# A two-layer trunk with a top-2-of-8 expert layer: the large experts' down products go from split fp32r to plain fp32, and scatters and split buffers are rearranged

## The chip, the cores and the metric

The kernel runs on one core of a Trainium2 chip. The metric is the device time of one execution in microseconds; the kernel before took 1336.89 us in the median of three runs (1332.23 to 1337.15). TensorE (PE in the profile) does the matmuls, ScalarE (ACT) and VectorE (DVE) move and change data between PSUM and SBUF, GpSimd (POOL) does little here, and SyncE (SP) issues the DMAs that fetch the weights from HBM.

## The reference, cut to what matters

Two layers over 256 frames of width 1024. The first is a mixer and a dense SwiGLU, the second an attention and a layer of eight experts, of which each frame uses two. Only the expert layer matters here:

```python
def swiglu(x, w1, w3, w2):
    return (jax.nn.silu(x @ w1) * (x @ w3)) @ w2

def moe_swiglu(xn, w_router, w1, w3, w2):
    logits = (xf @ w_router).astype(jnp.float32)
    vals, idx = lax.top_k(logits, TOP_K)                  # TOP_K = 2
    gates = jax.nn.softmax(vals, axis=-1)
    ...
    for e in range(N_EXPERTS):                            # 8; w1, w3: 1024 x 2816, w2: 2816 x 1024
        y = y + combine[:, e:e + 1] * swiglu(xf, w1[e], w3[e], w2[e])
```

Everything is float32. The three matrices of an expert are 34.6 MB, the eight experts 277 MB.

## The kernel before

**Experts, slots and phases.** The kernel orders the experts in a sequence q = 0 to 7. An even q has room for 128 frames ("big", 128 slots), an odd one for 64 ("small"); frames beyond that would be done in a loop at the end. The hidden width of 2816 is done in two halves of 1408. A big expert takes them one after the other, as two phases, a small one together in one, so there are 12 phases n = 0 to 11: q0 in phases 0 and 1, q1 in 2, q2 in 3 and 4, q3 in 5, and so on to q7 in 11. `up n` is the gate and up products of a phase (w1 and w3, 16 steps j), `down n` its down products (w2). TensorE works in the order up 0, up 1, down 0, up 2, down 1, up 3, down 2, up 4, and so on: the down stage of a phase comes after the up stage of the next. One pair of experts, big and small, is six stages: up (raw, small), down (big, second half of the expert before), up (big, first half), down (small), up (big, second half), down (big, first half).

**Two ways to multiply.** A big expert's products are made of three single-pass fp32r matmuls each (`product`, L462 to L464): weights and activations are split into a high part (a copy to fp32r) and the rest. ScalarE writes the high part of a weight piece (`split_step_hi`, L713), VectorE the rest (`split_step_lo`, L1658), into one of three buffers `w_hi`, `w_lo` of 2048 columns. A piece of step v is split behind step v - 3, in both engines' written order. A small expert's products are plain fp32 matmuls on the raw piece in the ring, on half of the array's columns each, two beside each other (L1487, L1511).

**The ring of weights.** Two arenas of SBUF, 10240 and 12288 columns, 11.5 MB together, hold pieces of weights in the order of their use. SyncE issues one DMA a piece (`load_step`, L535) as soon as the space is free: for a piece that was split, when VectorE has split it (`lo_done`); for a raw one, when TensorE has used it (`raw_used`). An up piece is 1408 columns in a big phase (704 KB, 0.721 MB) and 2816 in a small one, a down piece 2048 columns, two blocks of w2 (1.049 MB; the last of a half 1024 columns).

**Around the products.** After an up stage ScalarE makes the silu (`silu_up`, L953) and VectorE multiplies (`gate_up`, L2063); then TensorE turns the 11 blocks of activations (`turn_up`, L1445) and ScalarE and VectorE take them to SBUF. This happens within the down stage that follows; its places ("hooks") stand at every second block. `gather` (L1433) collects the frames of the next expert. `way_back` (L1454) turns the matrix of gates, VectorE copies it (`back_out`, L2081), and `scatter` (L1469) spreads an expert's result over the frames, which VectorE adds to `h` (`add_out`, L2098). Each engine works strictly in its written order, and waits on semaphores.

Of the kernel before, what the change touches and what calls it, by code (L numbers as in the profile page):

```python
# [14 lines left out]
P = 128  # L15
EPS = 1e-6
Step = namedtuple("Step", "kind n q a j hook part size big at ends")
# [4 lines left out]
def trunk(nc, x, e_norm1, e_w_in, e_sgu_ln_g, e_sgu_ln_b, e_sgu_w, e_sgu_b, e_conv_w, e_a_log,  # L22
# [90 lines left out]
    STEPS, n_big, n_raw = [], 0, 0  # L113
    for kind, n in WORK:
        q, a = PHASE[n]
        if kind == "up":
            todo = [Step(kind, n, q, a, j, None, (j // 2, j % 2), HALF if big(q) else FF, big(q), 0, False) for j in range(2 * DC)]
        else:
            todo = []
            for half in ((a,) if big(q) else (0, 1)):  # L120
                for j in range(0, HB, 2):
                    at = len(todo)
                    hook = at if big(q) else at // 2 if at % 2 == 0 else None
                    todo.append(Step(kind, n, q, half, at, hook, (j, min(2, HB - j)), min(2, HB - j) * D, big(q), 0, False))
        todo[-1] = todo[-1]._replace(ends=True)
        for st in todo:
            STEPS.append(st._replace(at=n_big if big(q) else n_raw))
            if big(q):
                n_big += 1
            else:  # L130
                n_raw += 1
# [5 lines left out]

    def place_pieces():

        dense_end = {}  # L140
        for i in range(A_MOE):
            dense_end[slot_of(i)] = i
        taken = [(slot * DC * CW, (slot + 1) * DC * CW, "unit", i) for slot, i in dense_end.items()]
        at = slot_of(A_MOE) * DC * CW
        arena = 0 if at < ARENAS[0][1] else 1
        where = []
        for st in STEPS:
            if at + st.size > ARENAS[arena][1]:
                arena = 1 - arena
                at = ARENAS[arena][0]  # L150
            lo, hi = at, at + st.size
            over = [x for x in taken if x[0] < hi and lo < x[1]]
            taken = [x for x in taken if not (x[0] < hi and lo < x[1])]
            for x in over:
                if x[0] < lo:
                    taken.append((x[0], lo, x[2], x[3]))
                if hi < x[1]:
                    taken.append((hi, x[1], x[2], x[3]))
            units = max([x[3] + 1 for x in over if x[2] == "unit"], default=0)
            raws = max([x[3] + 1 for x in over if x[2] == "raw"], default=0)  # L160
            taken.append((lo, hi, "unit", A_MOE + st.at) if st.big else (lo, hi, "raw", st.at))
            where.append((lo, units, raws))
            at = hi
        return where
# [14 lines left out]
    def arrive_end(k):  # L179
        return arrive_base(k) + 16 * sum(arrive_sem(v) == k for v in range(len(STEPS)))  # L180

    seen_units = seen_raws = 0
    for v, st in enumerate(STEPS):
        seen_units, seen_raws = max(seen_units, WHERE[v][1]), max(seen_raws, WHERE[v][2])
        if v < ARRIVE:
            k = arrive_sem(v)
            assert k >= RING or seen_units > dense_last[k]
        else:
            old = STEPS[v - ARRIVE]
            assert (seen_units > A_MOE + old.at) if old.big else (seen_raws > old.at)  # L190
# [12 lines left out]
    with ExitStack() as ctx:  # L203
# [16 lines left out]
        ident = sb("ident", [P, P])  # L220
        ones = sb("ones", [P, P])
# [3 lines left out]
        blk_ones = sb("blk_ones", [P, P])  # L225
        before = sb("before", [P, P])
# [11 lines left out]
        w_hi = [sb(f"w_hi{i}", [P, PIECE], F32R) for i in range(SPLITS)]  # L238
        w_lo = [sb(f"w_lo{i}", [P, PIECE], F32R) for i in range(SPLITS)]
# [90 lines left out]
        m_hi = [put(f"m_hi{k}", [P, HB, P], F32R) for k in range(2)]  # L330
        m_lo = [put(f"m_lo{k}", [P, HB, P], F32R) for k in range(2)]
        assert end[0] <= nc.sbuf_usable_end
        m_raw = [over(odd_at + 4 * HALF * k)[0](f"m_raw{k}", [P, HB, P]) for k in range(2)]
# [3 lines left out]
        r2 = put("r2", [P, 8, TILES, NE])  # L337
        nat = put("nat", [P, 8, NE])
# [4 lines left out]
        assert end[0] <= masks_at + 3 * 4 * P  # L343
# [97 lines left out]
        MOE_SCAT = (5, 0, 1, 2)  # L441
# [26 lines left out]
        def _(sp):  # L468
# [47 lines left out]
            def load_step(v, st, e):  # L516
# [8 lines left out]
                if st.kind == "up":  # L525
                    c, w = st.part
                    cols = slice(st.a * HALF, (st.a + 1) * HALF) if st.big else slice(0, FF)
                    src = (o_moe_w1, o_moe_w3)[w][0][bass.ds(e, 1), c * P:(c + 1) * P, cols].rearrange("e p n -> p (e n)")
                    dst = in_ring(lo, st.size)
                else:  # L530
                    j, nb = st.part
                    rows = slice(st.a * HALF, (st.a + 1) * HALF)
                    src = o_moe_w2[0][bass.ds(e, 1), rows, :].rearrange("e (j p) d -> p (e j) d", p=P)[:, j:j + nb, :]
                    dst = in_ring(lo, st.size).rearrange("p (j d) -> p j d", j=nb)
# [3 lines left out]
            for v, st in enumerate(STEPS):  # L538
                if st.q not in expert_of:
                    if len(expert_of) == 1:  # L540
                        sp.wait_ge(order_ready, 1)
                    expert_of[st.q] = sp.value_load(order_i[0:1, st.q:st.q + 1], min_val=0, max_val=NE - 1)
                load_step(v, st, expert_of[st.q])
# [125 lines left out]
        def _(act):  # L669
# [38 lines left out]
            def split_step_hi(v):  # L708

                st, i = STEPS[v], A_MOE + STEPS[v].at  # L710
                act.wait_ge(ring_in[arrive_sem(v)], arrive_count(v))
                used(act, i - SPLITS)
                act.activation(w_hi[i % SPLITS][:, 0:st.size], in_ring(WHERE[v][0], st.size), ACT.Copy).then_inc(hi_done, 1)  # L713
# [213 lines left out]
            split_step_hi(0)  # L927
            split_step_hi(1)
            norm(3)
            split_step_hi(2)  # L930
# [4 lines left out]
            def gathered(q):  # L935

                for b in range(2):
                    act.wait_ge(gather_done, 2 * q + b + 1)
                    src = ps[:, gather_bank(q, b), :]
                    if big(q):  # L940
                        act.activation(xg_hi[:, 4 * b:4 * b + 4, :], src.rearrange("p (c n) -> p c n", c=4), ACT.Copy)\
                            .then_inc(xgh_ready, 1)
                    else:
                        act.activation(xg_raw[:, 4 * b:4 * b + 2, :], src[:, 0:2 * SMALL].rearrange("p (c n) -> p c n", c=2),
                                       ACT.Copy).then_inc(xgh_ready, 1)
# [9 lines left out]
            def turned_hi(n, parts=range(PARTS)):  # L955

                for b in parts:
# [3 lines left out]
                    if big(PHASE[n][0]):  # L961
                        dst = m_hi[n % 2][:, blocks[0]:blocks[-1] + 1, :]
                    else:
                        src, dst = src[:, 0:2, :], m_raw[n % 2][:, blocks[0]:blocks[0] + 2, :]
                    act.activation(dst, src, ACT.Copy).then_inc(hTh_ready, 1)

            def finished(q):
# [4 lines left out]
                else:  # L972
                    ins = act.activation(y_exp[SMALL:P, 0:512], ps[SMALL:P, 6, :], ACT.Copy)
# [3 lines left out]
            for v, st in enumerate(STEPS):  # L977
                if finished_before(st) is not None:
                    finished(finished_before(st))
                if st.kind == "up" and st.n == 1 and st.j == 0:  # L980
                    silu_up(0)
                    turned_hi(0, (0, 1))
                if st.kind == "up" and st.n == 1 and st.j == 4:
                    turned_hi(0, (2,))
                if st.kind == "down" and st.n + 1 < PHASES:
                    q = PHASE[st.n + 1][0]
                    if st.hook == 0:
                        silu_up(st.n + 1)
                    if st.hook == 1:
                        turned_hi(st.n + 1)  # L990
                    if st.hook == 2 and LAST[q] == st.n + 1 and q + 1 < NE:
# [18 lines left out]
            with act.If(n_more > 0):  # L1010
                with act.Fori(0, n_more) as it:
# [9 lines left out]
        def _(pe):  # L1021
# [426 lines left out]
            def way_back(q):  # L1448

                pe.wait_ge(gated_done, TILES * (q + 1))  # L1450
                if q:
                    pe.wait_ge(scat_added, 4 * (q - 1) + 1)
                for t in range(TILES):
                    last = pe.transpose(ps[0:SLOTS, 5, t * P:(t + 1) * P], sel_w[:, t, :], ident[:, :])  # L1454
                last.then_inc(back_done, 1)

            def scatter(q, parts=range(4)):
                pe.wait_ge(hTl_ready, TURN0 + PARTS * min(LAST[q] + 3, PHASES))
                pe.wait_ge(back_ready, q + 1)
                pe.wait_ge(y_act, q + 1)  # L1460
                pe.wait_ge(y_vec, q + 1)
                for m in parts:
                    t, hf = m // 2, m % 2
                    if big(q):
                        a, y = back[:, t, :], y_exp[:, hf * 512:(hf + 1) * 512]
                    else:
                        rows = slice(hf * SMALL, (hf + 1) * SMALL)
                        a, y = back[rows, t, :], y_exp[rows, 0:512]
                    mm(ps[:, MOE_SCAT[m], :], a, y, start=True, stop=True).then_inc(scat_done, 1)  # L1469

            def up_step(v, st):

                (c, w), o = st.part, 3 * st.part[1]
                if st.big:
                    i = A_MOE + st.at
                    pe.wait_ge(lo_done, i + 1)
                    hi, lo = w_hi[i % SPLITS], w_lo[i % SPLITS]
# [743 lines left out]
```

## Time and profile before

| | |
|---|---|
| median of three runs | 1336.89 us |
| profiled execution, its own time | 1333.27 us |
| its span on the core | 1331.4 us |
| granted TensorE clock, mean | 0.964 |
| TensorE busy | 1216.3 us (91%) |
| VectorE, ScalarE busy | 691.6, 558.0 us |
| from HBM | 349.93 MB, 264 GB/s over the span |
| expert layer, from its first gather to its last product | 558.7 to 1319.2 us |

The expert layer takes 57% of the span. Its DMAs run at 420 to 430 GB/s where they are not held up. Busy shares are averages over stages with different limits, so the stages are read one by one.

### The profile page before, as it was taken

How to read it: one execution, taken by the hardware profiler on the slowest of the kernel's cores; microseconds unless marked ns; L12 is line 12 of the kernel's file. 1: busy time of each engine (PE TensorE's matmuls, PEld its weight loads, DVE VectorE, ACT ScalarE, POOL GpSimd, SP SyncE). 2: the span in 40 equal slices, each digit the busy share in tenths (PEclk: the TensorE clock that was granted, in tenths of full speed). 3: DMA queues.
4: the chain of work that ended last, by engine and by line, in shares of the span. 5: the costliest groups of instructions: out<-in, count | busy, mean ns of one | idle time of the engine just before them, and what ended most of it. 6: DMA issues, size and time to landing. Idle time of an engine off the chain costs nothing.

```text
span 1331.4 us, 15638 instructions
## 1 busy us (share of the span) xinstructions
PE 1216.3 (91%) x6391; PEld 906.7 (68%) x6391; DVE 691.6 (52%) x738; ACT 558.0 (42%) x597; POOL 52.6 (4%) x89
## 2 busy tenths in 40 slices
PE   6999899999999999788897998988998979999976
PEld 5899777888879987677735747537667457486352
DVE  4875545444454454587605848226567046484052
ACT  4661235433444565366404637125455035372041
POOL 7000000000000023000000000000000000000000
PEclk9999789999998999898998999999999989999989
DMA  9521219755553430186699999699997899995992
GB/s 309 175 92 47 96 32 371 235 174 185 190 182 125 153 131 19 63 280 241 239 404 420 363 395 417 266 424 392 354 419 316 343 420 371 368 404 197 426 419 120
DMA packets 107708, 352.05 MB, mean 264 GB/s; under 512 B 7072, under 2 KB 54192, under 8 KB 99440
## 3 DMA queue, kind: packets, MB, share of 16 engines
q1 hardware_dynamic: 106336, 347.11, 68.8%
q0 software_dynamic: 1296, 3.90, 1.0%
q8 instruction: 52, 0.85, 0.3%
q14 instruction: 24, 0.20, 0.0%
HBM read 349.93 MB, written 1.05 MB: 264 GB/s over the span
## 4 chain that ended last, share of the span: by engine, by line
PE 79%; DVE 8%; DMA 7%; ACT 3%; POOL 2%; issue 1%; POOLq 0%; DVEq 0%; ACTq 0%; SPq 0%
PE ps L462 17%; PE ps L463 17%; PE ps L464 17%; PE ps L1487 7%; PE ps L1511 6%; DMA arena_c<-in_o_moe_w_dram 5%; DVE w_lo L1658 4%; PE ps L1433 2%; ACT w_hi L713 2%; PE ps L1469 2%; PE ps L1445 2%; DMA arena_a<-in_o_moe_w_dram 1%; DVE u_act L2063 1%; PE ps L1360 1%; PE ps L1206 1%
## 5 line engine op out<-in xcount | busy, mean ns | idle before, releaser
L1658 DVE TENSOR_TENSOR w_lo<-arena_c,w_hi 128x1408 fp32r<-128x1408 f32 (+2 forms) x96 | 170.0, 1778 | 199.4 <-ACT w_hi L713 199.3
L713 ACT ACTIVATE w_hi<-arena_c 128x1408 fp32r<-128x1408 f32 (+2 forms) x96 | 144.8, 1509 | 228.9 <-DMA arena_c<-in_o_moe_w_dram 154.7
L1658 DVE TENSOR_TENSOR w_lo<-arena_a,w_hi 128x1408 fp32r<-128x1408 f32 (+2 forms) x80 | 138.1, 1732 | 93.1 <-ACT w_hi L713 93.1
L713 ACT ACTIVATE w_hi<-arena_a 128x1408 fp32r<-128x1408 f32 (+2 forms) x80 | 117.5, 1469 | 130.9 <-PE ps L464 67.3
L462 PE MATMUL ps<-w_hi,xg_hi 128*128 128x512 f32 (+1 forms) x384 | 147.2, 383 | 10.3 <-DVE back L2081 6.4
L463 PE MATMUL ps<-w_lo,xg_hi 128*128 128x512 f32 (+1 forms) x384 | 145.7, 379 | 0.0
L464 PE MATMUL ps<-w_hi,xg_lo 128*128 128x512 f32 (+1 forms) x384 | 144.9, 377 | 0.0
L462 PE MATMUL ps<-w_hi,x_hi 128*128 128x512 f32 (+1 forms) x336 | 125.7, 374 | 1.9 <-ACT xn L800 1.7
L464 PE MATMUL ps<-w_hi,x_lo 128*128 128x512 f32 (+1 forms) x336 | 122.9, 366 | 0.0
L463 PE MATMUL ps<-w_lo,x_hi 128*128 128x512 f32 (+1 forms) x336 | 122.8, 366 | 0.0
L1651 DVE TENSOR_TENSOR w_lo<-arena_a,w_hi 128x2048 fp32r<-128x2048 f32 x40 | 91.5, 2290 | 46.9 <-ACT w_hi L706 46.9
L462 PE MATMUL ps<-w_hi,m_hi 128*128 128x512 f32 x176 | 77.6, 441 | 19.6 <-DVE w_lo L1658 19.6
L462 PEld LDWEIGHTS ps<-w_hi,xg_hi 128*128 128x128 f32 x384 | 73.0, 190 | 26.5 <-issue 10.1
L1487 PE MATMUL ps<-arena_c,xg_raw 128*64 128x512 f32 (+1 forms) x432 | 87.5, 558 | 2.8 <-DMA arena_c<-in_o_moe_w_dram 2.8
L706 ACT ACTIVATE w_hi<-arena_a 128x2048 fp32r<-128x2048 f32 x40 | 76.5, 1912 | 27.6 <-PE ps L464 23.9
L462 PE MATMUL ps<-x_hi,w_hi 128*128 128x256 f32 x288 | 83.7, 291 | 3.7 <-DVE x_lo L1644 3.7
L1651 DVE TENSOR_TENSOR w_lo<-arena_c,w_hi 128x2048 fp32r<-128x2048 f32 x25 | 57.3, 2293 | 52.3 <-ACT w_hi L706 52.3
L464 PE MATMUL ps<-x_hi,w_lo 128*128 128x256 f32 x288 | 82.7, 287 | 0.0
L463 PE MATMUL ps<-x_lo,w_hi 128*128 128x256 f32 x288 | 82.7, 287 | 0.0
L464 PEld LDWEIGHTS ps<-w_hi,xg_lo 128*128 128x128 f32 x384 | 73.1, 190 | 11.7
L463 PEld LDWEIGHTS ps<-w_lo,xg_hi 128*128 128x128 f32 x384 | 73.1, 190 | 11.6
L1487 PE MATMUL ps<-arena_a,xg_raw 128*64 128x512 f32 x336 | 69.4, 560 | 6.1 <-DMA arena_a<-in_o_moe_w_dram 6.1
(349 smaller groups left out, 1904.6 us busy)
## 6 DMA issues: line engine op xcount, KB each, us to landing
arena_c<-in_o_moe_w_dram SPq DMA_DIRECT2D x36, 1408.0 KB, 9.9
arena_c<-in_o_moe_w_dram SPq DMA_DIRECT2D x69, 704.0 KB, 9.4
arena_c<-in_o_moe_w_dram SPq DMA_DIRECT2D x46, 1024.0 KB, 9.6
arena_a<-in_o_moe_w_dram SPq DMA_DIRECT2D x59, 704.0 KB, 8.8
arena_a<-in_o_moe_w_dram SPq DMA_DIRECT2D x28, 1408.0 KB, 8.9
arena_a<-in_o_moe_w_dram SPq DMA_DIRECT2D x34, 1024.0 KB, 9.2
arena_c<-in_e_ffn_w_dram SPq DMA_DIRECT2D x36, 512.0 KB, 4.8
arena_a<-in_e_ffn_w_dram SPq DMA_DIRECT2D x30, 512.0 KB, 4.8
```

The source lines that it names most:

```text
L462: pe.matmul(o, a_hi, b_hi, start=first, stop=False)
L463: pe.matmul(o, a_hi, b_lo, start=False, stop=False)
L464: return pe.matmul(o, a_lo, b_hi, start=False, stop=last)
L706: act.activation(w_hi[i % SPLITS][:, :], ring[slot][:, :], ACT.Copy).then_inc(hi_done, 1)
L713: act.activation(w_hi[i % SPLITS][:, 0:st.size], in_ring(WHERE[v][0], st.size), ACT.Copy).then_inc(hi_done, 1)
L1433: last = mm(ps[:, gather_bank(q, c // 4), at:at + n], xn[:, t, c * P:(c + 1) * P], sel_p[:, t, 0:n], start=(t == 0), stop=(t == TILES - 1))
L1445: last = pe.transpose(ps[:, turn_bank(n, b), i * P:(i + 1) * P], u_act[:, j * P:(j + 1) * P], ident[:, :])
L1469: mm(ps[:, MOE_SCAT[m], :], a, y, start=True, stop=True).then_inc(scat_done, 1)
L1487: last = mm(ps[a * SMALL:(a + 1) * SMALL, o + b, 0:n], xg_raw[:, c, :], raw[:, a * HALF + c0:a * HALF + c0 + n], start=(c == 0), stop=(c = ...
L1511: last = mm(ps[hf * SMALL:(hf + 1) * SMALL, 6, :], m_raw[st.n % 2][:, j, st.a * SMALL:(st.a + 1) * SMALL], raw[:, k * D + hf * 512:k * D + ...
L1651: tt(w_lo[i % SPLITS][:, :], ring[slot][:, :], w_hi[i % SPLITS][:, :].bitcast(F32), ALU.subtract).then_inc(lo_done, 1)
L1658: tt(w_lo[i % SPLITS][:, 0:st.size], in_ring(WHERE[v][0], st.size), w_hi[i % SPLITS][:, 0:st.size].bitcast(F32), ALU.subtract).then_inc(lo ...
```

## The change

In words:

- The down products of big experts are one plain fp32 matmul on the raw piece, full width, in place of three on split parts. `m_hi`, `m_lo` go; the turned activations are copied once, by ScalarE, to `m_raw`. VectorE only passes the semaphore on.
- A down step is one block of w2 (j = 0 to 10 in a half), no longer two; a fetched down piece is still two. A small up piece is fetched as two DMAs of 704 KB, no longer one of 1408 KB.
- `w_hi` and `w_lo` are one area of 6144 columns each, which holds four pieces of 1408. Only up pieces of big experts are split. A table `BEHIND` says behind which step a split is issued: behind the step that used the piece whose buffer it takes, or, if that is later, behind the step that frees the ring space its own fetch needs.
- The turn stands at block 3 of a big down stage and block 5 of a small one, the gather at block 5.
- Scatters and ways back stand only in small down stages: for the big expert before, way back at block 7, scatters at 10 and 12; for the small expert before that, at 14, 17 and 19. Their PSUM banks change.
- The routing operations on VectorE in up 0 are spread over steps 2, 5, 8, 11, and part of them goes to up 2. The first turn stands at steps 3 and 7 of up 1, no longer at 0 and 4.

```diff
+            for half in (a,) if big(q) else (0, 1):
+                for j in range(HB):
+                    if j % 2 == 0:
+                        v = new_piece(kind, q, half, (j, min(2, HB - j)), min(2, HB - j) * D, False)
+                    todo.append(Step(kind, n, q, half, len(todo), j, D, False, 0, False, [(v, (j % 2) * D)]))
...
+        for s, st in enumerate(STEPS):
+            if not st.big:
+                continue
+            if at + st.size > SPLIT_ROOM:
+                at = 0
+            last = max(claim(taken, at, at + st.size, A_MOE + st.at))
+            spot[st.at] = (at, last)
+            raws = max(raws_needed[:st.pieces[0][0] + 1])
+            free = step_of.get(last, last - A_MOE)
+            if raws:
+                free = max(free, raw_step[raws - 1])
+            behind.setdefault(free, []).append(s)
+            at += st.size
...
-        MOE_SCAT = (5, 0, 1, 2)
+        SCAT = {q: (5, 4, 0, 1) if big(q) else (2, 5, 4, 0) for q in range(NE - 1)}
+        TURN_AT, GATHER_AT = {True: 3, False: 5}, 5
+        SCAT_AT = {0: ((10, (0, 1)), (12, (2, 3))), 1: ((17, (0, 1)), (19, (2, 3)))}
+        BACK_AT, LAST_BACK_AT = (7, 14), 20
...
-                            last = product(pe, ps[:, 6 + hf, :], m_hi[st.n % 2][:, j, :], m_lo[st.n % 2][:, j, :],
-                                           w_hi[i % SPLITS][:, cs], w_lo[i % SPLITS][:, cs],
-                                           st.a == 0 and j == 0, st.a == 1 and j == HB - 1)
+                (v, off), = st.pieces
+                pe.wait_ge(ring_in[arrive_sem(v)], arrive_count(v))
+                raw = in_ring(WHERE[v][0] + off, D)
+                for hf in range(2):
+                    if big(st.q):
+                        last = mm(ps[:, 6 + hf, :], m_raw[st.n % 2][:, j, :], raw[:, hf * 512:(hf + 1) * 512], start=first, stop=end)
+                        continue
...
                 if st.kind == "down" and st.n + 1 < PHASES:
-                    if st.hook == 0:
+                    if st.j == 0:
                         silu_up(st.n + 1)
...
-                if v + SPLITS < len(STEPS) and STEPS[v + SPLITS].big:
-                    split_step_hi(v + SPLITS)
+                for k in BEHIND.get(s, ()):
+                    split_step_hi(STEPS[k])
```

**Where instructions move.** First ScalarE, at the end of the raw up stage `up 5` (expert 3) and in the big down stage `down 4` behind it. `u_act` is the silu, `m_raw` the turned activations, `ring_in` the semaphore of a piece's arrival. Before:

```order
L713 ACTIVATE w_hi<-arena_a 128x2048 [waits piece_used,ring_in11]
L713 ACTIVATE w_hi<-arena_a 128x2048 [waits piece_used,ring_in12]
L713 ACTIVATE w_hi<-arena_c 128x2048 [waits piece_used,ring_in13]
L953 ACTIVATE u_act<-ps 128x512 [waits hT_done,raw_used]
L953 ACTIVATE u_act<-ps 128x512
L953 ACTIVATE u_act<-ps 128x384
```

Now:

```order
L773 ACTIVATE all_hi<-arena_c 128x1408 [waits piece_used,ring_in13]
L773 ACTIVATE all_hi<-arena_c 128x1408 [waits piece_used,ring_in14]
L773 ACTIVATE all_hi<-arena_c 128x1408 [waits piece_used,ring_in15]
L773 ACTIVATE all_hi<-arena_c 128x1408 [waits piece_used,ring_in16]
L1015 ACTIVATE u_act<-ps 128x512 [waits hT_done,raw_used]
L1015 ACTIVATE u_act<-ps 128x512
```

Three splits of pieces of `down 4` stood ahead of the silu; now four splits of pieces of `up 6` do. VectorE's order there is the same with its own halves of the splits and the gating. The six pieces of `down 4` are fetched ahead of those four.

Second VectorE, in the small down stage `down 5`. `back` is the turned matrix of gates, `h` the additions behind a scatter. Before:

```order
L2063 TENSOR_TENSOR u_act<-u_act,ps 128x384 [waits silu_done]
L2073 TENSOR_TENSOR m_lo_59<-ps,m_hi_57 128x512 [waits hTh_ready] x2
L2073 TENSOR_TENSOR m_lo_59<-ps,m_hi_57 128x384 [waits hTh_ready]
L2098 TENSOR_TENSOR h<-h,ps 128x512 [waits scat_done] x4
L1658 TENSOR_TENSOR w_lo<-arena_a,w_hi 128x1408 [waits hi_done]
L2081 COPY back<-ps 128x256 [waits back_done]
```

Now:

```order
L2125 TENSOR_TENSOR u_act<-u_act,ps 128x384 [waits silu_done]
L2040 TENSOR_SCALAR sel_w<-iota,tab 128x128 x2
L1714 TENSOR_TENSOR all_lo<-arena_c,all_hi 128x1408 [waits hi_done]
L1714 TENSOR_TENSOR all_lo<-arena_c,all_hi 128x1408 [waits hTh_ready,hi_done]
L1714 TENSOR_TENSOR all_lo<-arena_c,all_hi 128x1408 [waits hi_done]
L2137 COPY back<-ps 128x256 [waits back_done]
L1714 TENSOR_TENSOR all_lo<-arena_c,all_hi 128x1408 [waits hi_done]
L2154 TENSOR_TENSOR h<-h,ps 128x512 [waits scat_done] x4
```

The three splits ahead of `back` are of pieces whose ring space is freed by blocks 3, 5 and 5 of this same stage; before, the scatter of the big expert came ahead of any split, with a `back` made in the stage before.

## Rows read from the trace of the kernel before

**Rows 1.** The page's busy times: us, share of the span, instructions.
```profile
PE 1216.3 (91%) x6391; PEld 906.7 (68%) x6391; DVE 691.6 (52%) x738; ACT 558.0 (42%) x597; POOL 52.6 (4%) x89
```
**Rows 2.** Windows: length, busy PE, PEld, DVE, ACT, POOL, clock, DMA share, GB/s; by pair.
```profile
662.65:850.42 187.77, 173.05 (x820) 110.95 (x818) 96.86 (x86) 76.27 (x68) 0.00 (x0) 0.98 0.93 377
850.42:1037.34 186.92, 173.78 (x820) 113.18 (x821) 96.91 (x86) 76.77 (x68) 0.00 (x0) 0.97 0.92 371
1037.34:1225.42 188.08, 175.38 (x819) 114.53 (x821) 96.32 (x84) 76.79 (x68) 0.00 (x0) 0.96 0.91 361
1225.42:1319.20 93.78, 82.98 (x369) 37.51 (x369) 19.93 (x22) 13.74 (x14) 0.00 (x0) 0.96 0.82 339
```
**Rows 3.** The third pair's windows: up 8 (raw), down 7, up 9, down 8 (small), up 10, down 9.
```profile
1037.34:1080.35 43.01, 38.16 (x192) 13.57 (x193) 2.29 (x1) 3.73 (x2) 0.00 (x0) 1.00 0.93 384
1080.35:1108.52 28.17, 23.93 (x111) 19.55 (x112) 18.37 (x20) 15.11 (x17) 0.00 (x0) 0.88 1.02 421
1108.52:1140.93 32.41, 32.41 (x144) 27.52 (x144) 23.52 (x17) 18.02 (x13) 0.00 (x0) 0.95 0.95 350
1140.93:1166.13 25.20, 25.20 (x111) 8.62 (x110) 10.42 (x16) 7.07 (x9) 0.00 (x0) 1.00 0.94 374
1166.13:1197.75 31.62, 30.97 (x146) 26.37 (x145) 25.53 (x17) 23.02 (x17) 0.00 (x0) 1.00 1.01 410
1197.75:1225.42 27.67, 24.72 (x119) 18.90 (x121) 16.18 (x17) 9.85 (x12) 0.00 (x0) 0.94 0.57 211
```
**Rows 4.** PE's waits from 556 us on (total, times, longest); timeline rows with idle time.
```profile
PE ps L1445 <- DVE u_act L2063: 23.9, 9, 4.9
PE ps L462 <- DVE w_lo L1658: 23.5, 10, 4.3
PE ps L462 <- DVE back L2081: 6.4, 3, 2.2
...
573.82 0.50 PE L462 MATMUL ps<-w_hi,xg_hi 128*128 128x512 f32 x1 [1.91 <-DVE w_lo L1658]
...
604.20 1.97 PE L1445 MATMUL ps<-ident,u_act 128*128 128x128 f32 x8 [4.85 <-DVE u_act L2063]
```
**Rows 5.** The chain that ended last, third pair: start, us, what.
```profile
1037.34 28.52 PE ps L1487 x144
...
1066.00 15.06 DMA arena_a<-in_o_moe_w_dram
...
1085.32 1.67 DVE u_act L2063 x3
...
1091.67 0.23 PE ps L463
...
1092.83 3.57 PE ps L1433 x32
```
**Rows 6.** fp32 matmuls: L1271's row (starts of first and last), and chain rows.
```profile
L1271 PE MATMUL ps<-rn,ones x4: 593/593/593, 177.2 to 178.5; 128*128 128x512 f32 x4
...
1031.89 1.06 PE ps L1469 x4
...
1152.10 1.91 PE ps L1469 x4
1154.01 3.58 PE ps L1511 x16
```
**Rows 7.** ScalarE's timeline at the third down piece; DMA of the window 1092 to 1108.
```profile
1081.09 1.91 ACT L713 ACTIVATE w_hi<-arena_a 128x2048 fp32r<-128x2048 f32 x1 [0.65 <-DMA arena_a<-in_o_moe_w_dram]
...
DMA packets 1359, 6.79 MB, mean 425 GB/s; under 512 B 153, under 2 KB 153, under 8 KB 1359
```
**Rows 8.** In down 8: landing of pieces into arena_c; a split on ACT and DVE.
```profile
DMA to landing us min/median/max: 5.1/6.5/8.2
...
1155.00 1.38 ACT L713 ACTIVATE w_hi<-arena_c 128x1408 fp32r<-128x1408 f32 x1 [0.38 <-DMA arena_c<-in_o_moe_w_dram]
...
1160.15 1.62 DVE L1658 TENSOR_TENSOR w_lo<-arena_c,w_hi 128x1408 fp32r<-128x1408 f32 x1
```

More of the change, by code:

```diff
@@ L16 @@
 EPS = 1e-6
-Step = namedtuple("Step", "kind n q a j hook part size big at ends")
+Step = namedtuple("Step", "kind n q a j part size big at ends pieces")
+Piece = namedtuple("Piece", "kind q a part size big last")
 EXP_LN = "natural_log_exp_and_others"
@@ L136, in trunk, with claim @@
     ARRIVE = 18
+    def claim(taken, lo, hi, mark):
+        over = [x for x in taken if x[0] < hi and lo < x[1]]
+        left = [x for x in taken if not (x[0] < hi and lo < x[1])]
+        for x in over:
+            if x[0] < lo:
+                left.append((x[0], lo, x[2]))
+            if hi < x[1]:
+                left.append((hi, x[1], x[2]))
+        taken[:] = left + [(lo, hi, mark)]
+        return [x[2] for x in over]
     def place_pieces():
@@ L146, in place_pieces @@
         where = []
-        for st in STEPS:
-            if at + st.size > ARENAS[arena][1]:
+        for pc in PIECES:
+            if at + pc.size > ARENAS[arena][1]:
                 arena = 1 - arena
                 at = ARENAS[arena][0]
[L151 to L163, printed above, removed]
+            old = claim(taken, at, at + pc.size, (pc.big, (A_MOE if pc.big else 0) + pc.last))
+            units = max([i + 1 for unit, i in old if unit], default=0)
+            raws = max([i + 1 for unit, i in old if not unit], default=0)
+            where.append((at, units, raws))
+            at += pc.size
         return where
@@ L179, in arrive_end @@
     def arrive_end(k):
-        return arrive_base(k) + 16 * sum(arrive_sem(v) == k for v in range(len(STEPS)))
+        return arrive_base(k) + 16 * sum(arrive_sem(v) == k for v in range(len(PIECES)))
     seen_units = seen_raws = 0
-    for v, st in enumerate(STEPS):
+    for v, pc in enumerate(PIECES):
         seen_units, seen_raws = max(seen_units, WHERE[v][1]), max(seen_raws, WHERE[v][2])
@@ L329, in trunk @@
         put, end = over(odd_at)
-        m_hi = [put(f"m_hi{k}", [P, HB, P], F32R) for k in range(2)]
-        m_lo = [put(f"m_lo{k}", [P, HB, P], F32R) for k in range(2)]
+        m_raw = [put(f"m_raw{k}", [P, HB, P]) for k in range(2)]
         assert end[0] <= nc.sbuf_usable_end
-        m_raw = [over(odd_at + 4 * HALF * k)[0](f"m_raw{k}", [P, HB, P]) for k in range(2)]
         put, end = over(masks_at)
@@ L337, in trunk @@
         r2 = put("r2", [P, 8, TILES, NE])
+        assert end[0] <= before_at
+        put, end = over(before_at)
         nat = put("nat", [P, 8, NE])
@@ L342, in trunk @@
         order_i = put("order_i", [1, 8], I32)
-        assert end[0] <= masks_at + 3 * 4 * P
+        assert end[0] <= level_at
+        y_small = over(ones_at)[0]("y_small", [P, 512])
+        back_last = over(level_at)[0]("back_last", [SLOTS, TILES, P])
         table = tab[:, 0:6, :].rearrange("p (k t) n -> p k t n", t=TILES)
@@ new lines, in down_step @@
+            def down_step(st):
+                j = st.part
+                first, end = st.a == 0 and j == 0, st.a == 1 and j == HB - 1
+                (v, off), = st.pieces
+                pe.wait_ge(ring_in[arrive_sem(v)], arrive_count(v))
+                raw = in_ring(WHERE[v][0] + off, D)
[3 more added lines that the diff above has]
+                        continue
+                    last = mm(ps[hf * SMALL:(hf + 1) * SMALL, 6, :], m_raw[st.n % 2][:, j, st.a * SMALL:(st.a + 1) * SMALL],
+                              raw[:, hf * 512:(hf + 1) * 512], start=first, stop=end)
```

345 lines of the change are left out of this document (181 added, 164 removed).

## Prediction

> **What bounds the kernel now.** I read four views. First the page's busy times: TensorE is busy for 91% of the span [rows 1], so whatever leaves it idle or gives it more to do is the time. Then the windows of the expert part, cut where TensorE starts the gate and up products of a 64-slot expert: three stretches of 187.8, 186.9 and 188.1 us, each one pair of experts, and a last one of 93.8 us [rows 2]. Then one such pair by stage [rows 3]. The reader is to see two things there. TensorE idles in four of the six stages (43.01 - 38.16, 28.17 - 23.93, 31.62 - 30.97, 27.67 - 24.72: 12.7 us in all), and its granted clock is below 1 in three: 12% of 28.2, 5% of 32.4 and 6% of 27.7 us are 6.7 us. The DMA share is 0.93 to 1.02 in the first two stages and 0.57 in the last, so the transfers limit only around the 64-slot expert. Last the waits: for the gated activation 23.9 us, for VectorE's half of a split 23.5, for the copy `back` 6.4 [rows 4]. The chain shows where the longest of these come from: a piece issued at 1066.00 lands 15 us later, is split by ScalarE and VectorE, and only then are the activations gated and turned [rows 5].
>
> A pair needs 69.2 MB of weights. At the 425 GB/s of a saturated stretch [rows 7] that is 163 us, so memory alone doesn't bound a pair, before or after.
>
> **TensorE's work.** The down products of the four 128-slot experts are 4 x 22 blocks x 2 column halves = 176 products. Before, each is three single-pass matmuls of 0.233 us (the 0.23 of [rows 5]; its neighbours show 0.23 and 0.24), 0.70 us. Now each is one fp32 matmul, which the trace counts as two instructions. Full-width fp32 rows: four instructions of L1271 start within 1.3 us, 0.433 us apart; in L1469, between matmuls on 64 columns, four take 1.91 us, 0.478 each [rows 6]. I take 0.44, near the pure stream: 0.88 a product, 1.76 us a block, 19.4 us for a half where it was 15.4. That is 352 x 0.44 - 528 x 0.233 = +31.9 us; the two ends are 352 x 0.433 (+29.4) and 352 x 0.478 (+45.2). Gain or nothing is excluded, since both ends lie above 0.70.
>
> The Trainium skill (FP8 and Floating Point Precision, "TensorE Precision Notes") says that true FP32 takes four passes through the array. With a pass at the measured 0.233 us that would be 0.93 a product, +41 us in the sum, between my value and the upper end; the row of L1271, at 0.87, lies under it.
>
> **What goes with the splits.** After the up products of a 128-slot expert, ScalarE and VectorE no longer have three 2048-column pieces to split ahead of gating. The waits there (0.65 for the split, 2.9 for gating, in the stages at 1166 and 1197: [rows 3]) lose their cause; gating takes 1.7 us [rows 5], the silu before it about as long, and TensorE has three blocks, 5.3 us, before it turns. So -3.6 us a pair. The wait for `back` at the start of an up stage, 6.4 / 3 = 2.1 us [rows 4], goes with the way back that moved: -2.1. ScalarE and VectorE are under no load in a down stage now; that by itself is worth nothing.
>
> **The first new wait: gating behind four splits.** Up splits now run four pieces ahead and are issued behind the step that frees their ring space. For the 128-slot expert that follows a 64-slot one these are steps 12 to 14 of the raw up stage. In both engines' order four splits therefore stand ahead of the silu and the gating of the 64-slot expert, and each waits for its piece to land. These pieces are fetched after all six of the down stage in between, though TensorE needs them later. Queued behind them: silu, gating, the turn at block 3 of the down stage, and all of TensorE.
> A ledger from TensorE's start of the raw up stage (t = 0, 1037.34 in the trace): before, the third down piece is split from 1081.09 on [rows 7], t = 43.7. By then 16 x 1.442 + 3 x 1.049 = 26.2 MB must have arrived, of which 7 pieces (10.1 MB) fit in the ring at t = 0; 16.1 MB in 43 us against 384 GB/s x 43 = 16.5 in the stage [rows 3]. So the ledger holds. Now the fourth up piece is what counts: 23.07 + 5.77 (six down pieces) + 4 x 0.721 = 31.7 MB, of which the finer pieces let 15 x 0.721 = 10.8 MB in at t = 0. The rest flows from the first freed step (2.4 us): 2.4 + 20.9 / 0.425 = 51.6, landed at 52.1. ScalarE's split 1.4, VectorE's 1.6 [rows 8], gating 1.7: the turn can start at 56.9. TensorE gets there at 16 x 2.377 (28.52 us for 144 instructions, 12 a step, [rows 5]) + 5.3 = 43.3. It waits 13.6 us, where it now loses about 7 (0.62, 4.24 and 2.13, the 0.62 and 4.24 as 43.01 - 38.16 in [rows 3]). The clock falls in it as now: 3.4 us (12% of 28.17). Bounds: nothing, if pieces were there; 20 us, if the ring is not full at t = 0.
>
> **The second new wait: `back` behind two splits.** In the 64-slot down stage the way back of the 128-slot expert stands at block 7, the first scatter at block 10. VectorE's copy `back` stands behind the splits of pieces whose space is freed by blocks 3 and 5 of this very stage. With the turn (1.4 us), block 5 ends 0.895 x 6 + 1.4 = 6.8 us in (16 instructions of a block's kind in 3.58 us are four blocks: [rows 6]). Two pieces then are issued; the first lands 6.5 us later [rows 8], the second 1.7 after it (0.721 MB at 425 GB/s): 15.0. Split 1.4 and 1.6, copy 0.4: 18.4. TensorE reaches block 10 at 0.895 x 10 + 1.4 + 0.4 = 10.7: 7.7 us of waiting, and 1.7 for the clock (as 6% of 27.67, [rows 3]). Bounds: 4.6 with the shortest landing of [rows 8], 5.1 us, and no second piece behind it; nothing, if the splits found their pieces; above, 9.
>
> **The sum.** One pair from t = 0: raw up 38.0; down 5.3 + 13.6 + turn 1.4 + eight blocks 14.1 + gather 3.5 [rows 5] + clock 3.4, to 79.3; up 30.9; 64-slot down 19.7 + 1.4 + ways back 0.8 + scatters 3.8 and 2.1 (two each of 1.91 and 1.06, [rows 6]) + 7.7 + 1.7, to 147.4; up 30.9; down 19.4 + 1.4 + 3.5: 202.6 us against 187.6. Three pairs: +45.0. The first has one scatter and way back fewer: -2.5. The last stretch has no split to wait for and the DMA has the ring full: 38.0 + 20.8 + 26.8 + 0.4 = 86.0 against 93.8: -7.8. Start of the expert part: the first turn waits 4.85 us now and moves three steps later (-3, with its clock); two waits of 1.9 for splits [rows 4], with the routing operations spread, -2; the first down stage +4.0 - 3.6: together -4.6. The 64 more DMAs of 704 KB cost nothing: such pieces already move at 425 GB/s [rows 7], and SyncE issues them inside its waits; bounds 0 to 2 us. Sum +30.1, from 1333.3 to 1363.4. The median of the runs shown is 3.6 above that execution; I add a part of that and say 1364.
>
> The skill's page DMA: Bandwidth & Descriptors ("Rules for kernel authors") asks for at least 1 MiB in a DMA. By it the halved pieces would be slower. The trace's 704 KB pieces at 425 GB/s do not bear it out, so it gets no chance of its own.
>
> **Rivals.**
> - *Dear fp32 matmuls.* 0.478 us an instruction as between the tiled ones: +13, 1376. For it: the only fp32 rows with changing weights in this part; against it: half of each row's surroundings are another tiling.
> - *Only the first wait.* If the copy `back` is in time (the two pieces land early or the scatter finds VectorE free), 3 x 9.4 us less: 1336, no change. For it: landing is measured on other traffic; against it: the order of VectorE.
> - *Neither wait, the faster side.* If at t = 0 the DMA is some 3.7 MB further on, so that the fourth up piece has landed at 43 and not at 52, gating is in time as well: another 3 x 17.0 less, 1285. It decides from where the four pieces land before TensorE has done three blocks. Against it: the ring's 11.5 MB are full already in my ledger.
>
> **How the numbers follow.** This kernel's measurement can tell 0.5% from no change, 6.7 us. Forecast with both waits 0.60; dear matmuls on top 0.14; only the first wait 0.14 (a third each slower, same, faster, as its sizes scatter); neither 0.12. Slower 0.60 + 0.14 + 0.04 = 0.78, same 0.06, faster 0.16. The range leaves out the 1285 case and the top of the dear one: 1318 to 1388. The likeliest case by itself: 1350 to 1378.
>
> **What would show it.** After a raw up stage: four splits on ScalarE, then silu; a TensorE wait for gating of 12 to 15 us, three times, and none after 128-slot up stages. In the 64-slot down stage: a TensorE wait of 5 to 9 us at the first scatter, for `back`. fp32 down instructions 0.43 to 0.48 us apart. Last stretch 86 us. Wrong would be: the ledger, if the pieces land before 50; the price, if a half takes over 21 us; or a saving I don't see, if TensorE's sum of idle time falls.

## The result and the profile after

| | before | after |
|---|---|---|
| median | 1337.02 us (4 runs) | 1374.37 us (4 runs, 1373.72 to 1375.95) |
| profiled execution, its span | 1331.4 us | 1372.6 us |
| granted TensorE clock, mean | 0.964 | 0.951 |

The ratio is 1.0306, with a 95% interval of 1.0282 to 1.033: the change makes the kernel 3.1% slower. The forecast was 1364 us, with a range of 1318 to 1388. The line numbers below are those of the changed kernel: `product` is L523 to L525, the raw up products L1549, the down products of a 128-slot expert L1562 and of a 64-slot one L1564, the turn L1506, the gather L1494, the scatter L1531; the splits are L773 (ScalarE) and L1714 (VectorE), silu L1015, gating L2125, the copy `back` L2137, SyncE's DMAs L595. In the experiments the same lines stand a few numbers further on (the turn is L1509 in e2, L1512 in e3).

The page's busy row of after, answering to [rows 1] (us, share of the span, instructions):

```profile
PE 1237.1 (90%) x6215; PEld 868.4 (63%) x6215; DVE 574.1 (42%) x646; ACT 475.2 (35%) x549; POOL 52.6 (4%) x89
```

VectorE and ScalarE lost 117 and 83 us of work, and nothing came of it: neither sets the time by its busy share. TensorE got 21 us more, and the span 41. The other half must be idle time.

Windows of after, cut where TensorE starts a 64-slot expert's up products, answering to [rows 2] (length; busy PE, PEld, DVE, ACT, POOL; clock, DMA share, GB/s):

```profile
654.44:860.81 206.37, 178.76 (x765) 103.72 (x767) 63.85 (x54) 55.94 (x56) 0.00 (x0) 0.93 0.86 337
860.81:1066.25 205.44, 180.00 (x775) 103.83 (x777) 67.87 (x63) 56.11 (x56) 0.00 (x0) 0.93 0.84 337
1066.25:1271.50 205.25, 179.32 (x776) 103.72 (x776) 67.34 (x61) 56.12 (x56) 0.00 (x0) 0.94 0.87 339
1271.50:1360.30 88.80, 85.96 (x358) 31.73 (x357) 10.56 (x21) 3.53 (x7) 0.00 (x0) 1.00 0.87 357
```

The three pairs take 617.1 us where they took 562.8 (+54.3). The expert part's first pair starts 8.2 us earlier (654.44 for 662.65), and the last stretch is 5.0 shorter. Less was moved per us (337 to 339 GB/s for 361 to 377): memory waited too.

The second pair by stage, in the order of [rows 3] (up raw, down, up, down small, up, down; the rows of before are its third pair, which is as long as its second within 1.2 us):

```profile
860.81:899.90 39.09, 38.29 (x193) 13.82 (x193) 0.00 (x0) 0.00 (x0) 0.00 (x0) 1.00 1.01 412
899.90:944.20 44.30, 26.40 (x88) 14.79 (x89) 9.98 (x11) 9.74 (x12) 0.00 (x0) 0.77 0.73 286
944.20:975.20 31.00, 31.00 (x146) 26.28 (x147) 20.19 (x13) 17.47 (x14) 0.00 (x0) 1.00 1.02 409
975.20:1010.20 35.00, 28.25 (x113) 9.16 (x111) 15.11 (x21) 7.98 (x10) 0.00 (x0) 0.90 0.67 261
1010.20:1041.00 30.80, 30.80 (x146) 25.57 (x143) 20.23 (x14) 17.22 (x13) 0.00 (x0) 1.00 1.02 420
1041.00:1066.25 25.25, 25.25 (x97) 14.21 (x97) 2.35 (x5) 3.70 (x8) 0.00 (x0) 1.00 0.60 224
```

Four stages have length equal to busy time, or nearly. All of the loss stands in two: the down stage behind the raw up stage (44.3 us for the 28.2 of [rows 3]) and the small down stage (35.0 for 25.2).

TensorE's waits from 556 us on, answering to [rows 4] (engine, line waited for: total, times, longest):

```profile
PE ps L1506 <- DVE u_act L2125: 52.2, 3, 17.9
PE ps L1531 <- DVE back L2137: 21.9, 3, 8.2
PE ps L1549 <- DMA arena_a<-in_o_moe_w_dram: 4.0, 5, 0.9
PE ps L523 <- ACT u_act L1015: 2.9, 1, 2.9
```

Twenty-two short and middling waits (23.9 + 23.5 + 6.4 us) have gone, but for one of 2.9 us, and six long ones have come: three of about 17.4 us for the gating, three of about 7.3 for `back`. The chain of the second pair shows the first (start, us, what):

```profile
900.95 17.42 DMA arena_c<-in_o_moe_w_dram
...
918.39 1.39 ACT all_hi L773
...
919.80 1.62 DVE all_lo L1714
921.43 1.67 DVE u_act L2125 x3
...
923.14 2.61 PE ps L1506 x11
```

ScalarE's timeline there shows who stands in front of whom (in brackets the idle time before, and what ended it; two of the four splits are left out):

```profile
913.38 1.38 ACT L773 ACTIVATE all_hi<-arena_c 128x1408 fp32r<-128x1408 f32 x1 [62.51 <-DMA arena_c<-in_o_moe_w_dram]
...
918.39 1.38 ACT L773 ACTIVATE all_hi<-arena_c 128x1408 fp32r<-128x1408 f32 x1 [0.31 <-DMA arena_c<-in_o_moe_w_dram]
919.68 1.44 ACT L1015 ACTIVATE u_act<-ps 128x512 f32<-128x512 f32 x3
```

ScalarE has been idle for 62.5 us, 13.5 of them after the up stage ended at 899.90 and the silu's input was complete. The silu isn't late because ScalarE is busy, but because four splits stand ahead of it in the written order, each waiting for a piece that TensorE needs only a stage later. In the small down stage VectorE's timeline shows the same with `back`:

```profile
986.26 1.62 DVE L1714 TENSOR_TENSOR all_lo<-arena_c,all_hi 128x1408 fp32r<-128x1408 f32 x1 [8.41 <-ACT all_hi L773]
988.88 3.16 DVE L1714 TENSOR_TENSOR all_lo<-arena_c,all_hi 128x1408 fp32r<-128x1408 f32 x2 [0.99 <-ACT all_hi L773]
991.96 0.42 DVE L2137 COPY back<-ps 128x256 f32<-128x256 f32 x1
```

Three splits stand ahead of `back`, as the order listing has it. The chain to it, in the same stage, which TensorE starts at 974.86:

```profile
978.68 6.15 DMA arena_c<-in_o_moe_w_dram
...
986.14 1.03 ACT m_raw L1023 x2
...
987.46 1.40 ACT all_hi L773
...
988.88 3.16 DVE all_lo L1714 x2
992.04 0.34 DVE back L2137
```

### The profile page after: what moved, and what is told of

The parts are those of the page before. It is cut to its first block, busy times and chain, and to the rows that moved or that the text cites. A ratio compares the mean times of both kernels' runs of the same rounds, so it can differ in the third digit from the quotient of the medians.

```text
span 1372.6 us, 15350 instructions
## 1 busy us (share of the span) xinstructions
PE 1237.1 (90%) x6215; PEld 868.4 (63%) x6215; DVE 574.1 (42%) x646; ACT 475.2 (35%) x549; POOL 52.6 (4%) x89
## 4 chain that ended last, share of the span: by engine, by line
PE 80%; DMA 9%; DVE 4%; ACT 2%; POOL 2%; SPq 1%; issue 1%; POOLq 0%; DVEq 0%; ACTq 0%
PE ps L523 15%; PE ps L525 15%; PE ps L524 15%; PE ps L1562 10%; PE ps L1549 7%; PE ps L1564 5%; DMA arena_a<-in_o_moe_w_dram 5%; DMA arena_c<-in_o_moe_w_dram 4%; PE ps L1494 2%; PE ps L1531 2%; SPq L595 1%; PE ps L1506 1%; DVE all_lo L1714 1%; PE ps L1421 1%; PE ps L1267 1%
## 5 line engine op out<-in xcount | busy, mean ns | idle before, releaser
L1714 DVE TENSOR_TENSOR all_lo<-arena_a,all_hi 128x1408 fp32r<-128x1408 f32 x60 | 97.0, 1623 | 168.9 <-ACT all_hi L773 168.0
L1714 DVE TENSOR_TENSOR all_lo<-arena_c,all_hi 128x1408 fp32r<-128x1408 f32 x68 | 110.0, 1623 | 100.9 <-ACT all_hi L773 100.7
L523 PE MATMUL ps<-all_hi,xg_hi 128*128 128x512 f32 (+1 forms) x384 | 146.4, 381 | 2.9 <-ACT u_act L1015 2.9
L524 PE MATMUL ps<-all_lo,xg_hi 128*128 128x512 f32 (+1 forms) x384 | 144.4, 376 | 0.0
L525 PE MATMUL ps<-all_hi,xg_lo 128*128 128x512 f32 (+1 forms) x384 | 143.8, 374 | 0.0
L773 ACT ACTIVATE all_hi<-arena_a 128x1408 fp32r<-128x1408 f32 x60 | 82.8, 1383 | 174.7 <-DMA arena_a<-in_o_moe_w_dram 147.4
L773 ACT ACTIVATE all_hi<-arena_c 128x1408 fp32r<-128x1408 f32 x68 | 94.0, 1386 | 113.4 <-DMA arena_c<-in_o_moe_w_dram 72.2
L523 PE MATMUL ps<-all_hi,x_hi 128*128 128x512 f32 (+1 forms) x336 | 125.9, 375 | 1.9 <-ACT xn L860 1.7
L524 PE MATMUL ps<-all_lo,x_hi 128*128 128x512 f32 (+1 forms) x336 | 123.2, 367 | 0.0
L525 PE MATMUL ps<-all_hi,x_lo 128*128 128x512 f32 (+1 forms) x336 | 123.1, 366 | 0.0
L1562 PE MATMUL ps<-arena_c,m_raw 128*128 128x512 f32 x208 | 94.8, 606 | 0.2 <-DMA arena_c<-in_o_moe_w_dram 0.2
L1549 PE MATMUL ps<-arena_c,xg_raw 128*64 128x512 f32 (+1 forms) x408 | 92.3, 558 | 1.6 <-DMA arena_c<-in_o_moe_w_dram 1.6
L523 PE MATMUL ps<-x_hi,all_hi 128*128 128x256 f32 x288 | 84.1, 292 | 3.9 <-DVE x_lo L1700 3.9
L1549 PE MATMUL ps<-arena_a,xg_raw 128*64 128x512 f32 x360 | 83.0, 559 | 4.0 <-DMA arena_a<-in_o_moe_w_dram 4.0
L766 ACT ACTIVATE all_hi<-arena_a 128x2048 fp32r<-128x2048 f32 x40 | 76.5, 1912 | 27.8 <-PE ps L525 23.9
L523 PEld LDWEIGHTS ps<-all_hi,xg_hi 128*128 128x128 f32 x384 | 72.1, 188 | 18.2 <-ACT u_act L1015 3.2
L525 PE MATMUL ps<-x_hi,all_lo 128*128 128x256 f32 x288 | 82.9, 288 | 0.0
L524 PEld LDWEIGHTS ps<-all_lo,xg_hi 128*128 128x128 f32 x384 | 72.1, 188 | 12.1 <-issue 0.7
L525 PEld LDWEIGHTS ps<-all_hi,xg_lo 128*128 128x128 f32 x384 | 72.1, 188 | 11.5
```

The lines of the kernel that those rows point to most:

```text
L523: pe.matmul(o, a_hi, b_hi, start=first, stop=False)
L524: pe.matmul(o, a_hi, b_lo, start=False, stop=False)
L525: return pe.matmul(o, a_lo, b_hi, start=False, stop=last)
L766: act.activation(w_hi[i % SPLITS][:, :], ring[slot][:, :], ACT.Copy).then_inc(hi_done, 1)
L773: act.activation(unit(all_hi, st), in_ring(WHERE[v][0] + off, st.size), ACT.Copy).then_inc(hi_done, 1)
L1562: last = mm(ps[:, 6 + hf, :], m_raw[st.n % 2][:, j, :], raw[:, hf * 512:(hf + 1) * 512], start=first, stop=end)
```

## The experiments

**e1, the first wait alone.** In the planner, a split that would stand behind a step of a raw up stage goes behind block 6 of the down stage that follows, so behind silu and gating:

```diff
+            f = STEPS[free] if free >= 0 else None
+            if f is not None and f.kind == "up" and not f.big:
+                free = next(k for k in range(free, len(STEPS)) if STEPS[k].kind == "down") + 6
             behind.setdefault(free, []).append(s)
```

> The four splits that stood ahead of the silu of a 64-slot expert now stand behind block 6 of the 128-slot down stage that follows. If their place in ScalarE's and VectorE's order is the cause, the three waits of TensorE for gating (52.2 us in all) go, and with them the low clock (0.77 over the 44.3 us of that stage): the stage falls to 24.3 us, three times 20 less, 1314 us. If in truth the transfers set the pace, the wait only moves to the next up stage, whose pieces land when they landed before: 1360 to 1374.

Measured: 1322.5 us (5 runs), a ratio to before of 0.9912 [0.9884, 0.994]. The wait for gating is gone. Of TensorE's waits the longest is now:

```profile
PE ps L1534 <- DVE back L2140: 29.6, 3, 10.0
```

So moving these splits alone gives back 52 us and leaves the kernel 0.9% faster than before. The expectation was 8 us too low: the wait for `back` grew from 21.9 to 29.6. The DMAs that its three chains lead back to take 9.40, 9.22 and 9.14 us here, and 7.61, 6.15 and 6.30 in the changed kernel: 7.7 us more together, and that is what the waits grew by. Why they take longer is a reading: the long first wait had given memory time to run ahead of TensorE, and without it more pieces are under way when these are issued.

**e2, the second wait alone.** Splits that would stand behind one of blocks 0 to 13 of a small down stage go behind block 14:

```diff
+            f = STEPS[free] if free >= 0 else None
+            if f is not None and f.kind == "down" and f.q % 2 and f.j < 14:
+                free += 14 - f.j
             behind.setdefault(free, []).append(s)
```

> The splits that stood behind blocks 3, 5, 5 and 7 of the 64-slot down stages, ahead of the copy of the turned gates, now stand behind block 14. If their place is the cause, the three waits at the first scatter (21.9 us) go, and the low clock behind them (0.90 over 35 us): 1342 us. If the next up stage then finds its first splits late, under 10 us are left of it.

Measured: 1346.34 us (5 runs), ratio 1.0084 [1.0057, 1.0111]. No wait for `back` is left, and the other stays as it was:

```profile
PE ps L1509 <- DVE u_act L2128: 51.8, 3, 17.3
```

The second wait is worth 28 us with its share of the clock. The expectation was 4 us too low: it gave the clock 10% of the whole stage, 3.5 us a time, where 1.9 are lost (below).

**e3, both edits.**

> Both moves together. If the two waits are independent, their gains add: 1282 us, a pair of experts in 175 us, and this is faster than the kernel before. If memory then becomes the bound, a pair can't fall far under 175 to 180 and waits for pieces appear in the raw up stages: 1290 to 1310.

Measured: 1286.55 us (4 runs, 1284.6 to 1289.25), ratio 0.964 [0.9607, 0.9673]. This is faster than both kernels. The gains of e1 and e2 add up to 79.9 us, and both moves together give 87.8: the difference is the growth of the wait for `back` in e1, which has gone too. The windows of the three pairs, and then the chain of the second around the place where the first wait was:

```profile
655.09:829.90 174.81, 172.97 (x765) 101.34 (x764) 63.61 (x54) 55.83 (x56) 0.00 (x0) 1.00 0.98 398
829.90:1007.36 177.46, 175.90 (x774) 101.85 (x773) 67.45 (x63) 55.85 (x56) 0.00 (x0) 1.00 0.96 390
1007.36:1185.74 178.38, 175.78 (x775) 101.89 (x774) 66.84 (x61) 55.88 (x56) 0.00 (x0) 1.00 0.96 390
```
```profile
870.13 5.35 PE ps L1568 x12
875.47 1.20 PE ps L1512 x11
876.67 3.44 PE ps L1568 x8
```

A pair is 175 to 178 us, TensorE is busy for about 99% of it at full clock, and memory at 0.96 to 0.98 of its share. The turn, which took 2.61 us after the wait, takes 1.20. These rows also close the sum: the pairs are 86.4 us shorter than the changed kernel's 617.1, of which 74.1 are the waits; the other 12.3 are, within a microsecond, the clock after them (3 x 4.3 us, below).

**e4, a dose.** As e1, but one of the four splits (that of each up stage's first piece) stays ahead of the silu:

```diff
+            if f is not None and f.kind == "up" and not f.big and st.j:
```

> As the first of these, but one of the four splits stays ahead of the silu. If gating waits for the landing of the last piece split ahead of it, the wait ends when the first up piece lands, which the trace has 5.0 us before the fourth (913.4 against 918.4), and ends 1.6 us of VectorE's queue earlier at most: waits of 10.5 to 12.5 us in place of 17.4, some 1357 us. If the number of splits ahead, not the landing, sets it, three quarters of the wait go: 4 us, 1335.

Measured: 1358.88 us, a single run.

```profile
PE ps L1509 <- DVE u_act L2128: 36.3, 3, 12.3
```

12.1 us each for one split ahead, 17.4 for four. The difference is three landings of a piece at the memory's rate: 3 x 0.721 MB / 0.42 = 5.1 us (ScalarE's four splits above start 1.67 us apart). So it isn't the number of splits or their 1.4 us each, but when the last piece ahead of the silu lands, and even the first lands far too late.

**e7, TensorE given other work.** The splits stay where the change has them; in a big down stage the turn goes from block 3 to block 8 and the gather from 5 to 9:

```diff
-        TURN_AT, GATHER_AT = {True: 3, False: 5}, 5
+        TURN_AT, GATHER_AT = {True: 8, False: 5}, {True: 9, False: 5}
```

> The changed kernel with the big down stage's transposes put behind its eighth block instead of its third, and the gather of the next expert's tokens behind the ninth instead of the fifth; all splits stay where the change has them. If the wait is the time by which the gating vector comes (fourth up piece landed and split), TensorE has five more blocks of work before it needs the vector, 5 x 1.73 = 8.6 us by the profile after: the three waits fall from 17.4 to about 8.8 us each, 26 us less in all, a little of the clock's loss comes back, and up to 1 us a pair may be lost at the later gather: 1345 to 1348 us. If instead the vector comes later because TensorE frees the arena's space later (the work that follows the wait sets it), the waits stay near 17 us and the time at 1374.

Measured: 1349.31 us (4 runs), ratio 1.0107 [1.0075, 1.0138].

```profile
PE ps L1506 <- DVE u_act L2125: 27.4, 3, 9.3
PE ps L1531 <- DVE back L2137: 22.7, 3, 8.2
```

The gating comes when its piece lands, whatever TensorE does: five blocks of work shorten the wait from 17.4 to 9.1 us, 8.3 where 8.6 were expected, and the time is 1.3 us above the expected 1345 to 1348. That is half a cure; e1's is whole, since it takes away what gating stands behind.

**e5 and e6, the price of plain fp32.** On e3, the down products of the 128-slot experts are made of three single-pass fp32r matmuls (e5), or of one (e6), on a fixed tile instead of activations and weights. This leaves that part's computation out, but neither its DMAs nor its waits for them:

```diff
-                        last = mm(ps[:, 6 + hf, :], m_raw[st.n % 2][:, j, :], raw[:, hf * 512:(hf + 1) * 512], start=first, stop=end)
+                        m = fixed[:, 0:P]
+                        last = product(pe, ps[:, 6 + hf, :], m, m, fixed[:, :], fixed[:, :], first, end)
```

> The kernel with both moves, but the down products of the 128-slot experts are three single-pass fp32r matmuls again, on a fixed tile in place of the piece and the activations (so they are left out of the result); no split is added. Same operations otherwise. This is the price of plain fp32 by itself: 176 x (0.866 - 0.70) = 29 us if TensorE sets the pace, 1257 us. If memory takes over near 163 us a pair, some of it is lost: up to 1270. If TensorE does not set the pace, under 5 us change: 1282 to 1287.

> As the one before with one single-pass matmul in place of three, so TensorE has 111 us less than with plain fp32. It shows where memory takes over. If TensorE alone set the pace: 1176 us. If a pair cannot be shorter than its 69.2 MB at 425 GB/s (163 us, where the kernel with both moves has 175), only about 12 us a pair and a part of the last stretch are to be had: 1235 to 1250.

Measured: e5 1256.71 us (4 runs), ratio 0.9431 [0.9403, 0.9459]; e6 1242.35 us (4 runs), ratio 0.9317 [0.929, 0.9345]. From e3 to e5 it is 29.8 us: that is what 176 products in plain fp32 cost over three passes each, with no long wait beside them. The two were timed apart; by their ratios to before, each beside its own runs of it, it is 28 us, and the intervals leave some 6 either way. From e5 to e6 TensorE is given 176 x 2 x 0.233 = 82 us less to do, and the time falls by 14. Memory takes over, as the three pairs of e5 and of e6 together and the longest waits of e6 show:

```profile
647.42:1155.32 507.90, 501.86 (x2442) 329.36 (x2441) 198.70 (x178) 168.94 (x168) 0.00 (x0) 1.00 1.01 411
642.49:1139.64 497.15, 455.18 (x2179) 284.80 (x2178) 199.78 (x183) 168.35 (x168) 0.00 (x0) 0.98 1.02 419
```
```profile
PE ps L1557 <- DMA arena_c<-in_o_moe_w_dram: 15.3, 18, 1.9
PE ps L530 <- DVE all_lo L1722: 12.3, 3, 4.2
```

In e6 the DMA share is 1.02 over all three pairs and TensorE idles for 42 us of them: 165.7 us a pair, near the 163 that the prediction worked out from the bytes, is where memory sets the time here. e3, at 176.9 on the mean, stands 7% above it. Of these 11.2 us a pair e5 gets 7.6, with a DMA share of 1.01 and TensorE busy for 99%. Splitting again to save the 29 us would need VectorE and ScalarE to be late for nothing, which no run tried.

## Why the prediction was right, and where its sizes were off

**Direction and mechanism: right.** Both waits came where the working put them, three times each, behind the splits it named (three of them ahead of `back`; the working spoke of the last two), and e1 and e2 take each away alone. No wait for gating is left after a 128-slot up stage.

**The price of the fp32 matmuls: right.** The last six blocks of a half take this on the chain of after:

```profile
850.45 10.36 PE ps L1562 x24
```

24 instructions in 10.36 us, 0.432 each, 0.86 a product: 352 x 0.432 - 528 x 0.233 = +29.0 us, forecast +31.9, and e3 and e5 put it at 28 to 30. It is the lower end of the bounds, the row of L1271 in [rows 6]; the dearer row of that group, taken between matmuls on half of the columns, says nothing on a run of full-width ones. The Trainium skill (FP8 and Floating Point Precision, "TensorE Precision Notes") gives true FP32 four passes. At the 0.233 us of a single pass that would be 0.93 a product and +41 us in the sum; the row lies 7% under it.

**The first wait: right in kind, 3.8 us a time too small.** The step that was off is the ledger's starting point, "15 x 0.721 = 10.8 MB in at t = 0". The fourth piece was to land at t = 52.1; it landed at 918.39 - 860.81 = 57.6, and the wait was 17.4 us for 13.6. What arrived in that time is this window of after:

```profile
860.81:918.40 57.59, 43.64 (x204) 15.94 (x204) 3.53 (x3) 4.14 (x4) 0.00 (x0) 0.90 1.01 414
```

57.59 us x 414 GB/s are 23.8 MB. Of the 31.7 MB of the ledger about 7.9 were there at t = 0, not 10.8. The ring wasn't full. The two microseconds from t = 0 on show it, first before (third pair), then now (second pair). Before, nothing moves, since all that fits has landed; now the DMA engines are at work:

```profile
1037.34:1039.34 2.00, 2.00 (x10) 0.70 (x12) 0.00 (x0) 0.00 (x0) 0.00 (x0) 1.00 0.00 0
860.81:862.81 2.00, 2.00 (x10) 0.70 (x12) 0.00 (x0) 0.00 (x0) 0.00 (x0) 1.00 0.86 321
```

Of the last five pieces issued ahead of t = 0, three go out at 859.3 to 860.8 and land 4.5 to 6.2 us later. These are 2.2 MB still under way, most of the 2.9 that the ledger had too much:

```profile
852.25 8.91 SPq L595 DMA_DIRECT2D arena_c<-in_o_moe_w_dram  x5
```

What SyncE waits for in the down stage ahead of the raw up stage says why, before (1006:1037.34) and now (1041:1066.25):

```profile
SPq L535 <- DVE w_lo L1658: 24.0, 4, 12.1
SPq L595 <- PE ps L1562: 23.3, 5, 7.4
```

Before, VectorE's splits of the down pieces freed that space, up to three pieces ahead of TensorE; now only TensorE's use of a piece does. Taking the splits away also made the ring's space come free later. This part is read from the traces and the bytes; no run changed the ring alone. The forecast had it as its upper bound ("20 us, if the ring is not full at t = 0").

**The second wait: right in kind and size, in part by luck.** 8.2, 6.75 and 6.96 us for 7.7. In the second pair `back` is there 17.5 us into the stage, for 18.4, but by other terms. The forecast hung it on the landing of the second piece behind block 5, at 15.0. The chain above hangs on the piece issued behind block 3, which lands at 984.83, 10.0 us in; behind it ScalarE's copies of the turned activations (1.45 us) and two more splits follow without a gap, on pieces that have landed. The copies stand in no term of the sum, and the later landing that it had in their place made up for them.

**The clock: near in size.** The second pair again, around the two waits (same columns as the windows above; the second row lies within the first):

```profile
905.20:923.10 17.90, 0.04 (x1) 0.00 (x0) 8.15 (x7) 6.86 (x7) 0.00 (x0) 0.56 1.01 418
913.38:923.10 9.72, 0.00 (x0) 0.00 (x0) 8.15 (x7) 6.86 (x7) 0.00 (x0) 0.50 1.00 418
923.10:930.00 6.90, 6.86 (x19) 4.37 (x20) 0.00 (x0) 1.68 (x3) 0.00 (x0) 0.65 0.12 28
930.00:935.00 5.00, 5.00 (x36) 4.14 (x35) 1.13 (x2) 1.19 (x2) 0.00 (x0) 1.00 0.35 130
...
992.40:1000.00 7.60, 7.57 (x18) 2.42 (x20) 3.56 (x4) 0.00 (x0) 0.00 (x0) 0.75 0.06 24
1000.00:1010.20 10.20, 10.20 (x44) 2.95 (x46) 4.14 (x8) 0.00 (x0) 0.00 (x0) 1.00 0.79 296
```

The grant falls to one half, the lower of the two levels, while TensorE idles, which costs nothing, and stays low for a while once it works again, which does: 35% of 6.9 us are 2.4, and 25% of 7.6 are 1.9, where 3.4 and 1.7 were forecast. The stage's own 0.77 over 44.3 us would overstate it fourfold: a mean over a stretch with a long wait in it is not a cost.

**The sum.** Three pairs +54.3 us for the forecast's +42.5. The first wait's size is 3 x 3.8 = 11.4 of these 11.8; the smaller differences nearly cancel (raw up stages of 39.1 us for 38.0, against cheaper products and a smaller loss by the clock). The start gained 8.2 for 4.6: the two waits for gating and the three for splits there (7.8 and 4.5 us before) left one of 2.9. The last stretch gained 5.0 for 7.8: its raw up stage took 39.4 us for 38.0, with short waits for pieces, and its small down stage a little longer. Together +41.1 for +30.1, and 1374.4 for 1364.

**The rivals.** The dear matmul is out (0.432 us). Its number, 1376, is the closest to the result, for the wrong reason: a number that fits isn't a mechanism shown. That only the first wait comes is out by e2. "Neither wait" was 1285, and e3, which makes that case true by moving the splits, takes 1286.55. The model of a pair without waits was right; memory was not far enough ahead to make it so by itself.

**The piece size.** The Trainium skill (DMA: Bandwidth & Descriptors, "Rules for kernel authors") asks for at least 1 MiB in a DMA. From 913.38 on in the first wait (its row is above) only 704 KB pieces were on their way, at 418 GB/s and with the DMA engines' share at 1.00, so nothing was left for a larger piece to gain. In a queue that always holds several pieces (the one of the chain took 17.42 us from issue to landing) the rule isn't felt.

## What to carry to other kernels

A prefetch that is issued "as early as its space is free" is placed in an engine's instruction order too, and everything behind it waits for its landing. Ask of each such instruction what it stands in front of and who needs that, and put it behind the work whose input is ready already: here two rules in the planner turned a change of +3.1% into -3.6%. To find the case in a trace, look for an engine that is idle for a DMA while the input of an instruction further back in its order has long been there. When a consumer is removed that freed a buffer early, count again how full the ring is at each stage's start.

## What the runs showed of the hardware that was not expected

- The granted clock is at 0.50 for the first 4.8 us of work after a wait of 17.9 us and for the first 3.7 us after one of 6.75 us, and then at 1.00: the loss is 2.4 and 1.9 us. Per us of idling a long wait is cheap for the clock: 24.7 us of waiting go with 4.3 us of loss in the second pair, while before 12.7 us of idling went with up to 6.7 [rows 3].
- Removing one wait lengthened the next: that for `back` went from 21.9 to 29.6 us when the first was gone. That the pause of 17.4 us had been memory's lead is the reading given with e1, not shown by a run of its own.
- With 0.96 to 0.98 of the DMA share in use (398 and 390 GB/s a pair), TensorE lost about 1% of the time to missing pieces (3.5 + 2.5 + 1.1 us of such waits in all of e3's expert part).
